# Separate buffers for the first two weight chunks after a layer norm, and an earlier weight rounding in the attention's branch phase

## What is computed

```python
for l in range(2):                      # first block
    x = layer_norm(alpha * x + 0.5 * swiglu_ffn(x, ffn1_wi[l], ffn1_wo[l]), ...)
    x = layer_norm(alpha * x + mixer(x), ...)          # even or odd mixer
    x = layer_norm(alpha * x + 0.5 * swiglu_ffn(x, ffn2_wi[l], ffn2_wo[l]), ...)
for l in range(2):                      # second block
    o_a, o_b, o_m = three_attentions(rms_norm(x, ...))
    merged = gates[0] * (o_a @ w_br_a) + gates[1] * (o_b @ w_br_b) + gates[2] * (o_m @ w_br_m)
    x = x + rms_norm(merged @ w_out, ...)
    x = x + rms_norm(conv_ffn(rms_norm(x, ...)), ...)
```

## Time and profile before

| what | value |
|---|---|
| median of 3 runs | 3968.88 us (3968.82 to 3969.61) |
| profiled execution, its time | 3969.09 us |
| its span from first to last instruction | 3967.4 us |
| busy share PE / PE weight load | 93% / 76% |
| busy share DVE / ACT / POOL | 43% / 34% / 15% |
| mean granted TensorE clock | 0.958 of 2.4 GHz |

### The profile page before, as it was taken

One profiled execution on the slowest core, in us unless ns is written; L12 is line 12 of the kernel. 1 busy time (PEld: TensorE's weight loads), 2 busy tenths in 40 slices (PEclk: granted clock), 3 DMA queues, 4 the chain that ended last, 5 costly groups with the idle time before them and its releaser, 6 DMA issues. The chain is left out here.

```text
span 3967.4 us, 46155 instructions
## 1 busy us (share of the span) xinstructions
PE 3706.2 (93%) x18324; PEld 3014.1 (76%) x18324; DVE 1703.8 (43%) x2060; ACT 1368.3 (34%) x1828; POOL 612.7 (15%) x523
## 2 busy tenths in 40 slices
PE   8999987999999999887899989998999899998998
PEld 6888765888888888565788868776888687877886
DVE  2224463322422244753422254555664445547642
ACT  2223432322332243322322143344443423445432
POOL 2102002210311030130311041003111210012110
PEclk9999998999999999877999999998999999999999
DMA  3222211222222222000122233222222323222222
GB/s 138 95 90 80 92 52 43 88 100 89 94 85 100 87 93 85 28 1 17 70 95 89 95 114 111 103 70 88 95 95 91 116 101 117 77 93 85 95 89 81
DMA packets 62088, 340.09 MB, mean 86 GB/s; under 512 B 7024, under 2 KB 11520, under 8 KB 32768
## 3 DMA queue, kind: packets, MB, share of 16 engines
q1 hardware_dynamic: 61952, 338.19, 24.0%
HBM read 331.87 MB, written 6.29 MB: 85 GB/s over the span
## 5 line engine op out<-in xcount | busy, mean ns | idle before, releaser
L382 PE MATMUL bank<-x_hi,w_hi 128*128 128x512 f32 (+1 forms) x3680 | 1428.8, 388 | 144.2 <-POOL x_lo L2448 47.8
L383 PE MATMUL bank<-x_lo,w_hi 128*128 128x512 f32 (+1 forms) x3680 | 1411.3, 384 | 0.0
L384 PE MATMUL bank<-x_hi,w_lo 128*128 128x512 f32 (+1 forms) x3680 | 1410.6, 383 | 0.0
L351 DVE TENSOR_TENSOR w_lo<-raw,w_hi 128x2048 fp32r<-128x2048 f32 (+2 forms) x326 | 689.6, 2116 | 1000.2 <-ACT w_hi L346 999.6
L382 PEld LDWEIGHTS bank<-x_hi,w_hi 128*128 128x128 f32 x3680 | 708.3, 192 | 308.0 <-issue 102.3
L346 ACT ACTIVATE w_hi<-raw 128x2048 fp32r<-128x2048 f32 (+2 forms) x326 | 567.4, 1741 | 743.1 <-PE bank L384 737.5
L384 PEld LDWEIGHTS bank<-x_hi,w_lo 128*128 128x128 f32 x3680 | 707.0, 192 | 132.5
L383 PEld LDWEIGHTS bank<-x_lo,w_hi 128*128 128x128 f32 x3680 | 708.5, 193 | 129.5 <-issue 1.0
L382 PE MATMUL bank<-f_g_hi,w_hi 128*128 128x512 f32 (+1 forms) x770 | 287.7, 374 | 0.0
L384 PE MATMUL bank<-f_g_hi,w_lo 128*128 128x512 f32 (+1 forms) x770 | 285.6, 371 | 0.0
L383 PE MATMUL bank<-f_g_lo,w_hi 128*128 128x512 f32 (+1 forms) x770 | 285.6, 371 | 0.0
(11 more groups left out here) (427 smaller groups left out, 3467.7 us busy)
## 6 DMA issues: line engine op xcount, KB each, us to landing
raw<-in_weights SPq DMA_DIRECT2D x222, 1024.0 KB, 4.8
raw<-in_weights SPq DMA_DIRECT2D x96, 704.0 KB, 4.0
raw<-in_weights SPq DMA_DIRECT2D x8, 768.0 KB, 4.3
x_kept<-X SPq DMA_DIRECT2D x2, 2048.0 KB, 10.8
X<-x_kept SPq DMA_DIRECT2D x2, 2048.0 KB, 10.0
work<-in_rpb SPq DMA_DIRECT2D x12, 256.0 KB, 5.1
stats<-in_rpb SPq DMA_DIRECT2D x12, 256.0 KB, 5.2
X<-in_x SPq DMA_DIRECT2D x8, 256.0 KB, 6.2
```

What stands on the lines that cost most here:

```text
L351: dve.tensor_tensor(w_lo[:, s, 0:size], raw[:, s, 0:size], w_hi[:, s, 0:size].bitcast(F32), ALU.subtract).then_inc(lo_ready.sem, 1)
L382: pe.matmul(out, w_hi[:, s, w], hi(k), start=first and n == 0, stop=False, skip_group_check=not group)
L383: pe.matmul(out, w_hi[:, s, w], lo(k), start=False, stop=False, skip_group_check=not group)
L384: mm = pe.matmul(out, w_lo[:, s, w], hi(k), start=False, stop=last and n == len(kts) - 1, skip_group_check=not group)
```

## The change

- **Buffers of their own.** At the five boundaries the first two chunks of the next stage are rounded into buffers that PE does not use at that time, not into `w_hi` and `w_lo`. After a feed-forward these are tiles 11 to 18 of `g_hi` and `g_lo`; so that they are free in time, the last two output tiles take the second half of the contraction first (`last_tiles_together`, `half_tiles` over tiles 0 to 10), and the rounding waits for that (`gone`). In `mixer_out` they are new tiles, with padding tiles that place them.
- **Earlier rounding.** `early_hi` and `early_lo` do it. After a feed-forward the first chunk is rounded on ACT ahead of the squares of t = 0, its remainder made on DVE between the two residuals; the second chunk is done in the lead (ACT before the first tile, DVE after the third). In `mixer_out` both are rounded among the squares, and both remainders are made before the residuals of t = 0. The third chunk (`third_hi`, `third_lo`) goes into its ordinary slot at the end of the lead.
- **Order of the small matmuls.** `half_sums` of t = 0 now stands ahead of all t = 1 work, `half_stats` after three contraction tiles (9 matmuls) of it. In the lead, the small matmuls of t = 1 stand after all eight tiles of chunk n0. Three steps of the norm of t = 1 move back by some tiles.
- **`mixer_out`'s sums.** The provisional mean is taken from 2 tiles, and DVE subtracts it from the fourth tile on.
- **Attention.** ACT rounds the weight chunk of each pair of tiles first, ahead of `round_` of the even tile.

```diff
-    return pieces[[*range(n - 4), n - 4, n - 2, n - 3, n - 1]]
+    return pieces[[*range(n - 4), n - 3, n - 1, n - 4, n - 2]]
...
+        def early_hi(act, nb, c, v):
+            act.wait_ge(raw_loaded[c % 2], (c // 2 + 1) * 16)
+            act.wait_ge(chunk_used.sem, PRIME + nb.gone)
+            act.activation(nb.early[v][0], raw[:, c % 2, :], ACT.Copy).then_inc(hi_ready.sem, 1)
+
+        def early_lo(dve, nb, c, v):
+            dve.wait_ge(hi_ready.sem, PRIME + c + 1)
+            dve.tensor_tensor(nb.early[v][1], raw[:, c % 2, :], nb.early[v][0].bitcast(F32),
+                              ALU.subtract).then_inc(lo_ready.sem, 1)
+
+        def third_hi(act, c):
+            act.wait_ge(raw_loaded[c % 2], (c // 2 + 1) * 16)
+            act.wait_ge(chunk_used.sem, PRIME + c - 3)
+            act.activation(w_hi[:, c % 2, :], raw[:, c % 2, :], ACT.Copy).then_inc(hi_ready.sem, 1)
...
         # lead_vector (DVE)
-                    elif t == 0 and k == 1:
-                        one_chunk(split_lo, dve, n0)
+                    elif t == 0 and k == 2 and nb.one_early:
+                        early_lo(dve, nb, n0 + 1, 1)
+                    elif t == 0 and k == 4:
                         half_residual(dve, nb, 1, 1)
-                if t == 0:
-                    one_chunk(split_lo, dve, n0 + 1)
+            third_lo(dve, n0 + 2)
...
         # lead_scalar (ACT)
-            one_chunk(split_hi, act, n0)
+            if nb.one_early:
+                early_hi(act, nb, n0 + 1, 1)
...
-                        elif k == 5:
-                            one_chunk(split_hi, act, n0 + 1)
+            third_hi(act, n0 + 2)
...
         # lead_tensor (PE)
-                    if t == 0 and k == 2:
-                        half_sums(pe, nb, 1)
-                        half_stats(pe, nb, 1)
+                if t == 0:
+                    half_sums(pe, nb, 1)
+                    half_stats(pe, nb, 1)
...
         # half_tiles (PE)
+            half_sums(pe, nb, 0)
             for v, (s, at, ks) in enumerate(tiles):
-                out, n = bank[nb.banks[v]][:, HS:S], len(ks) // 2 + 2
+                out, n = bank[nb.banks[v]][:, HS:S], 3
...
                 if v == 0:
-                    half_sums(pe, nb, 0)
                     half_stats(pe, nb, 0)
...
         # mixer_out
-                            if 2 * j + 2 == BEFORE:
-                                shift_tensor(pe, acc)
+                            if j == 1:
+                                shift_tensor(pe, acc, 2)
...
-                        for k in range(BEFORE):
+                        for k in range(KT - 2):
                             square_scalar(act, k, accq, sq)
+                            if k >= KT - 4:
+                                early_hi(act, nb, n0 + n + k - KT + 4, k - KT + 4)
...
         # attend (ACT)
-                        for n in range(KT):
-                            if n + 3 < KT:
-                                open_gates(n + 3)
-                            if n % 2:
-                                at_chunk(split_hi, act, b0 + n // 2 + 2)
-                            round_(n)
+                        for j in range(NP):
+                            at_chunk(split_hi, act, b0 + j + 2)
+                            round_(2 * j)
+                            for n in (2 * j + 3, 2 * j + 4):
+                                if n < KT:
+                                    open_gates(n)
+                            round_(2 * j + 1)
```

More of the change, by code:

```diff
@@ L200 @@
     p: int
+    early: tuple = ()
+    gone: int = 0
+    one_early: bool = False
 class Chain:
@@ L375, in ahead, with wide @@
             return body
+        def wide(g, k):
+            return g[:, k:k + 4, :].rearrange("p a b -> p (a b)")
         def linear(pe, out, s, at, kts, hi, lo, first=True, last=True, group=True):
+            wh, wl = (w_hi[:, s, :], w_lo[:, s, :]) if isinstance(s, int) else s
             for n, k in enumerate(kts):
                 w = slice(at + n * P, at + n * P + P)
-                pe.matmul(out, w_hi[:, s, w], hi(k), start=first and n == 0, stop=False, skip_group_check=not group)
-                pe.matmul(out, w_hi[:, s, w], lo(k), start=False, stop=False, skip_group_check=not group)
-                mm = pe.matmul(out, w_lo[:, s, w], hi(k), start=False, stop=last and n == len(kts) - 1,
+                pe.matmul(out, wh[:, w], hi(k), start=first and n == 0, stop=False, skip_group_check=not group)
+                pe.matmul(out, wh[:, w], lo(k), start=False, stop=False, skip_group_check=not group)
+                mm = pe.matmul(out, wl[:, w], hi(k), start=False, stop=last and n == len(kts) - 1,
                                skip_group_check=not group)
@@ L435, in program, with third_lo @@
         halves = (slice(0, HS), slice(HS, S))
[L437 to L438 removed]
+        def early_hi(act, nb, c, v):
[10 more added lines that the diff above has]
+            act.activation(w_hi[:, c % 2, :], raw[:, c % 2, :], ACT.Copy).then_inc(hi_ready.sem, 1)
+        def third_lo(dve, c):
+            split_lo(dve, c - c % 2, 0, c % 2, CHUNK)
         def lead_vector(dve, n0):
@@ L531, in lead_tensor @@
                 for v in range(2):
-                    mm = linear(pe, bank[2 + v][:, halves[t]], (n0 + 1) % 2, v * KT * P, range(KT), xt, yt, group=False)
+                    mm = linear(pe, bank[2 + v][:, halves[t]], nb.early[1], v * KT * P, range(KT), xt, yt, group=False)
             mm.then_inc(chunk_used.sem, 1)
@@ L724, in half_scale, with sums_pool @@
             act.activation(rstd, rstd, ACT.Exp, scale=-0.5).then_inc(done.sem, 1)
-        def sums_pool(pool, acc, accq, sq, n=KT - 1):
-            for k in range(1, SHIFT):
+        def sums_pool(pool, acc, accq, sq, n=KT - 1, shift=SHIFT):
+            for k in range(1, shift):
                 pool.wait_ge(z_ready.sem, z_ready.at(k + 1))
@@ L767, in swiglu @@
                 c6 = n1 + 2 * KT - 4
-                nb = Boundary(l, which, 0.5 / ALPHA, (4, 5), (c6 + 2, c6 + 3), acc, accq, sq, 1 - norm[0].p if joined else 0)
+                nb = Boundary(l, which, 0.5 / ALPHA, (4, 5), (c6 + 2, c6 + 3), acc, accq, sq, 1 - norm[0].p if joined else 0,
+                              tuple((wide(g_hi, k), wide(g_lo, k)) for k in (FH, FH + 4)), c6 + 2, True)
                 with stage_block(joined) as block:
@@ L826, in _ @@
                             pe.wait_ge(z_ready.sem, z_ready.at(BEFORE - 1 + v))
-                            linear(pe, bank[4 + v][:, :], (c6 + v) % 2, 0, range(0, FH), g, h, last=False, group=False)\
+                            linear(pe, bank[4 + v][:, :], (c6 + v) % 2, 0, range(FH, FT), g, h, last=False, group=False)\
                                 .then_inc(chunk_used.sem, 1)
-                        half_tiles(pe, nb, [((c6 + v) % 2, 0, range(FH, FT)) for v in range(2)], g, h, False, c6 + 2)
+                        half_tiles(pe, nb, [((c6 + v) % 2, 0, range(0, FH)) for v in range(2)], g, h, False, c6 + 2)
                     @block.scalar
@@ L918, in _ @@
                         split2(BEFORE + 1, 0)
-                        for v in range(2):
-                            half_residual(dve, nb, 0, v)
+                        half_residual(dve, nb, 0, 0)
+                        early_lo(dve, nb, n1 + 2 * KT, 0)
+                        half_residual(dve, nb, 0, 1)
                     @block.gpsimd
@@ L953, in mixer_out @@
                 sums = sb(nm + "sums", [P, 2, S], F32, scope)
+                sb(nm + "below", [P, 14 * 256], F32, scope)
+                early_his = sb(nm + "early_hi", [P, 2, CHUNK], F32R, scope)
+                sb(nm + "between", [P, 28 * 256], F32, scope)
+                early_los = sb(nm + "early_lo", [P, 2, CHUNK], F32R, scope)
+                early = tuple((early_his[:, v, :], early_los[:, v, :]) for v in range(2))
                 acc, accq = sums[:, 0, :], sums[:, 1, :]
                 hi, lo = x_parts()
-                nb = Boundary(l, 1, 1.0 / ALPHA, (2, 3), (None, n0 + n - 1), acc, accq, sq, 1 - norm[0].p)
+                nb = Boundary(l, 1, 1.0 / ALPHA, (2, 3), (None, n0 + n - 1), acc, accq, sq, 1 - norm[0].p, early, n0)
                 with stage_block() as block:
@@ L998, in _ @@
                                     dve.wait_ge(chunk_used.sem, PRIME + n0 + j + 1)
-                                centre_vector(dve, 2 * j + v, 1.0 / ALPHA, bank[2 * (j % 2) + v])
-                        half_shift(dve, nb)
+                                centre_vector(dve, 2 * j + v, 1.0 / ALPHA, bank[2 * (j % 2) + v], 4, 2)
+                        half_shift(dve, nb, 2)
+                        for v in range(2):
+                            early_lo(dve, nb, n0 + n + v, v)
                         for v in range(2):
```

46 lines of the change are left out of this document (19 added, 27 removed).

## The result

The changed kernel takes 3907.64 us (median of 4 runs, 3906.92 to 3912.76) against 3969.03 us (3968.82 to 3969.61): ratio 0.9848, 95% interval 0.9831 to 0.9865. The forecast was 3910, the range 3888 to 3933. The profiled execution took 3906.92 us with a span of 3905.2 (before: 3969.09 and 3967.4), and the mean granted clock rose from 0.958 to 0.966.

What follows compares the result with a forecast made beforehand. PE, busy 93% of the span, was taken as the bound, through its waits and 1.2 GHz stretches. Terms 8.9 + 6.5 + 7.9 + 25.2 + 13.6 - 3.4 = 58.7 us off 3969.1 gave 3910, range 3888 to 3933.

Steps and rivals of the forecast that it cites:

- Mean after a feed-forward: Feed-forward boundary: mean of t = 0 arrives as before, since POOL's held sum makes PE wait 1.3 us.
- First and third tile of the lead: Feed-forward lead: PE waits 0.9 and 1.3 us at its start; third boundary saves 6.5 us, fourth 7.9, before clock charges.
- The first boundary: First boundary and even mixer behind it: 8.9 us saved, as the third chunk's remainder no longer delays eight DVE steps.
- Reading of the wait at 1085.71: Old third-boundary lead: second chunk's rounding delays the norm of t = 1 until PE waits 2.92 us.
- Mixer boundary: Second and fifth boundaries: POOL's last sum 681.0 against 685.3, PE's wait 5.8 us, 12.6 us saved each, 25.2 together.
- Attention: Two attention phases: weights rounded first end DVE's wait for them; 6.8 us saved each, 13.6 together.
- Clock: Three feed-forward boundaries: one short 1.2 GHz stretch each, costing 1.7 us; one falls away behind the first; net loss 3.4.
- POOL beside DVE: Rival, all boundaries and attentions: POOL gets in between or first, saving 22 us more, 3888; chance 0.15.
- Half given back: Rival: low clock at the front of `half_sums` and less from attention leave 37 us, 3932; chance 0.28 shared with two others.
- slower: Rival: new wait ahead of t = 1 leaves TensorE at 1.2 GHz for whole leads, 4005 us; chance 0.04.
- Raw chunks landing late: Rival, three boundaries: raw chunk 5 us late delays the mean of t = 0; 44 us saved, 3925; shared chance 0.28.
- Not reaching the end: Rival: DVE chains in mixer stages behind first and fourth boundaries absorb their gains; 42 us remain, 3927; shared chance 0.28.

Runs made afterwards that it cites:

- e12: Kernel before, with only ACT's square of the mean of t = 1 moved from after the lead's fifth tile to after its eighth: 3943.6 us, ratio 0.9936.
- e8: Changed kernel, but after a feed-forward both chunks are again rounded inside the lead, into buffers of their own: 3912.1 us, ratio 0.9853.
- e3: Changed kernel, but DVE's early weight remainders wait until POOL has made its last sum of t = 0: 3891.3 us, ratio 0.9806.

## Why the prediction was right, and where it was not

- **Mean after a feed-forward.** "No earlier": 12.36 us behind the block's start before (1065.71), 12.37 now (1046.57). The wait of 1.3 before the sums: 1.1 to 1.3.
- **First and third tile of the lead.** Forecast waits 0.9 and 1.3; measured 0.6, at the second tile and not at the first, and 1.46 at the third. The lead's end, at the third and the fourth boundary: 4.6 and 7.1 for 6.5 and 7.9 less 1.7 each for clock. At the fourth the stretch at 1.2 GHz that I charged did not come.
- **The first boundary.** Forecast 8.9, measured 7.1. PE's wait in the even mixer is 1.8 (forecast 2.0). The step that failed is the clock's: the new short stretch at 1.2 GHz came as charged (388.6), but the old one behind the lead did not fall away (415.9), so its 1.7 did not come back.
- **Reading of the wait at 1085.71.** Wrong, though the sum didn't suffer. I wrote that the second chunk's rounding "delays the norm of t = 1 until PE waits 2.92". It was the seventh tile of t = 0: ACT stood for the means from the fifth tile on (L716), then rounded, and DVE's remainder held POOL's for that tile, the first of two that end at 1085.66 and 1086.35:

```profile
1079.77 0.38 ACT L716 ACTIVATE stats<-bank 128x256 f32<-128x256 f32 x1 [3.69 <-PE bank L644]
...
1083.62 2.73 POOL L510 TENSOR_TENSOR x_lo<-X,x_hi 128x256 fp32r<-128x256 f32 x2 [1.87 <-ACT X L483]
```

  The walk let all tiles through at POOL's pace, which is right for either reading; but it gave the credit to early rounding. e12 shows that one moved step alone gives 27 us in the kernel before, of the 43 that the whole change takes out of the five boundaries, and e8 that the early rounding after a feed-forward gives 1.1 a boundary.
- **Mixer boundary.** Last POOL sum 4.6 earlier from the block's start (forecast 4.3), wait 5.6 (5.8), mean 3.2 earlier (2.5), 12.0 and 12.3 for 12.6. The number is nearer than the way to it, which is partly luck: the remainders hold one sum of POOL, not two, and what PE waits for in the end is the residual that stands behind them on DVE; POOL itself waits for it:

```profile
672.58 0.72 POOL L734 TENSOR_TENSOR o_sums<-o_sums,X 128x256 f32<-128x256 f32 x1 [2.65 <-DVE X L709]
```

- **Attention.** Forecast 6.8 a phase, measured 6.0 and 5.6 up to DVE's first remainder behind the phase. Up to the last weight remainder 6.7 had been gained (44.6 to 51.3 in the comparison of DVE's remainders); then 1.07 went, and POOL's last remainder, forecast 6.8 earlier, comes 5.6 earlier. Tile by tile the gains are 2.0, 2.0, 0.6 and 0.9, for 2.1, 2.1, 0.7 and 1.9: the term for tile 7 ("at 7 5.3 for 7.2") failed.

```profile
2657.42 2.29 DVE L354 TENSOR_TENSOR w_lo<-raw,w_hi 128x2048 fp32r<-128x2048 f32 x1
2659.62 1.75 DVE L3119 TENSOR_TENSOR work<-work 128x512 f32<-128x512 f32 x1
...
2662.12 1.27 POOL L3159 TENSOR_TENSOR x_lo<-work,x_hi 128x512 fp32r<-128x512 f32 x1 [1.29 <-ACT x_hi L2983]
```

  `join(7)`, 0.69 in the kernel before, takes 1.75, since POOL's remainder of tile 6, itself held by the weight remainder, goes first and holds DVE in turn.
- **Clock.** Forecast a loss of 3.4. In the boundaries 24 us at half clock are left of 61; elsewhere 243 of 271, which goes with 7.5 us that I had not forecast and can't explain. They cover the 4 us by which the sum of the terms was too high (58.7 for 54.7), and that the total came so near is to that extent luck.
- **Rivals.** POOL beside DVE (3888): refuted by the rows of 2.46 and 2.53, and by what e3 gains from keeping the two apart. Half given back, slower: no stretch at 1.2 GHz in a boundary is longer than 6.8 us, and at the fourth there is none. Raw chunks landing late: DVE's early remainder at the third boundary begins 6.28 behind the block's start (1040.48), forecast 6.25 (1059.6). Not reaching the end: the next stages start earlier by the whole gain. A rule of the Trainium skill ("SBUF — State Buffer", section "Who interferes with whom") says that an instruction of DVE with two SBUF inputs and one of GpSimd that reads SBUF exclude each other, the first holding the other for its whole length; the rows here agree, in both directions.

## What to carry to other kernels

Before a wait is given a cause, count the matmuls ahead of it and behind it: the count says which tile is awaited, the name of the releaser does not. A waiting instruction on an engine that also feeds PE (here ACT's square of the mean) belongs behind the steps that PE needs next. And a long DVE instruction on two SBUF tiles costs POOL up to its whole length: put it where POOL has nothing due, rather than cutting it up.
